# Three reorderings in a hybrid attention and ConvFFN step: page sums of two jobs, page maxima, convolution constants

## The chip, the cores and the metric

The kernel runs on one NeuronCore of a Trainium2 chip, in one launch. The metric is the device time of an execution in microseconds, as the median of several. The engines are named as the profile names them: PE is TensorE, PEld its weight loads, DVE is VectorE, ACT is ScalarE, POOL is GpSimd, SP is SyncE, which here issues all DMAs.

## What is computed

One decoder layer, for a prompt of 1024 tokens and for 8 single new tokens that attend to 1024 past positions each, in float32. The past keys and values lie in 128-row pages that a page table names.

```python
h = _rmsnorm(xp, attn_pre_g[l])
q1, q2, ka, va, qf, kf, vf, logf = _project(h, w_in[l], b_f[l], pos_p)   # rotary on q1, q2, ka
cf = jnp.cumsum(logf, axis=1)
oa, of = _prompt_attention(q1, q2, ka, va, qf, kf, vf, cf, lam)
# oa: (softmax(q1 k1^T) - lam * softmax(q2 k2^T)) v, causal, 4 heads
# of: softmax(q k^T + C[t] - C[s]) v, causal, 8 heads
xp = xp + _rmsnorm(_merge(oa, of, subln_g[l], lam_init, w_o[l]), attn_post_g[l])
xp, conv_p = _conv_ffn(xp, prev0, ffn_pre_g[l], w_gate[l], w_up[l], conv_w[l],
                       conv_b[l], w_down[l], ffn_post_g[l])
...
def _conv_ffn(x, prev, pre_g, w_gate, w_up, conv_w, conv_b, w_down, post_g):
    h = _rmsnorm(x, pre_g)
    g = h @ w_gate
    u = h @ w_up
    gp = jnp.concatenate([prev.astype(g.dtype), g], axis=1)
    c = conv_b
    for j in range(CONV_W):
        c = c + conv_w[j] * gp[:, j:j + S]
    a = jax.nn.gelu(c, approximate=True) * u
    out = a @ w_down
    return x + _rmsnorm(out, post_g), gp[:, -(CONV_W - 1):]
```

The 8 new tokens go through the same steps, with the pages' rows ahead of their own key and value.

## The kernel before

There are three phases: `project` (the input projection, the attention of the prompt and that over the pages), `merge` (output projection and norms) and `ffn`. Every float32 product of the dense layers is made from high and low parts, three products each (`w_hi`, `w_lo`, `ht_hi`, `ht_lo`). In each phase every engine has a program of its own, in a fixed order, and waits on semaphores. The order written in the loops is the order of execution on that engine, and whatever stands behind a waiting instruction waits too.

**The attention loop.** 64 jobs `J`: eight units (head pairs) `u = J // 8` by eight query tiles `t = J % 8`. Units 0 to 3 are the differential group, 4 to 7 the forgetting group (`fox`). A job's steps are spread over the next ones. In job J TensorE makes the scores of J (`scores_of`), one half chunk of a later unit's projection (`before`, twelve products of L1244), transposes of rows for the outputs (`rows_at`: values in tiles 0 and 1, "s" in tile 2, keys "k" in tiles 3 and 4), the weighted sum of J-2 (L1386, L1383), the small products for the page attention (`soft_at`), one or two value pages (L1428), a second half chunk in tiles 0 to 3 (`after`) and at last the transposes of job J-1's probabilities (`turn`, L1370). VectorE takes the maxima of job J's scores (`maximum`, L1103), scales and combines the probabilities of J-1 (`weights`, L1070 to L1079), scales the output rows of J-2 (`rows_out`, L1092, L1089), and does the page work. ScalarE makes the exponentials and copies results out of PSUM.

**The transposes' banks.** All small results of TensorE in this loop go in turn to two PSUM banks, in the order of the list `ring`. An entry may be written when the one two places before it has been copied out. `X` is an entry's place.

**The pages.** 64 key pages in 8 batches. SyncE loads page g (`load_key_page`, L493) into buffer g % 2 once page g-2 is summed (`red_done`); GpSimd multiplies it by the query (`multiply`, L634); VectorE sums it per head (`reduce_page`, L1027). Pages 9 and 10 have their products in job 5, page 11 in job 6, page 12 in job 7. `late_page` marks page 10, whose sum stands in job 7 behind the scaled rows. The others' sums stand at the end of a job, in `pages_and_norms`, with the maxima of a batch (`page_maxima`, L1033 and L1037) after its last page. In soft_at, "mt" transposes those maxima (L1402) one job later, "nm" spreads them to all partitions (L1405) the job after; "ls" sums the denominators (L1410), once, in job 59. VectorE answers with `row_maximum` and `shift`. "mt" falls in jobs 5, 12, 19, 26, 33, 40, 47 and 55, "nm" in the next ones.

**The ConvFFN.** For each of 22 column blocks f TensorE multiplies by gate and up weights. The first three (`PLAIN`) are plain, the rest go by seven half-size products that need sums and differences of the tokens (`token_sums`, on VectorE, spread over f = 0 to 2). Weights of f+1 are split by ScalarE (`split_hi`) and VectorE (`low_parts`). The convolution's taps, bias and state rows and the last norm's gains come as rows and are transposed on TensorE (L2524, L2526) into bank 6, and VectorE copies them out as `consts`.

Of the kernel before, what the change touches and what calls it, by code (L numbers as in the profile page):

```python
# [23 lines left out]
KC = D // P  # L24
# [12 lines left out]
FC = FF // P  # L37
# [125 lines left out]
def project(nc, io, place):  # L163
# [82 lines left out]
    PS = io["PS"]  # L246
# [33 lines left out]
    NJ = MAPS * NT  # L280
# [149 lines left out]
    with nc.Block() as block:  # L430
# [500 lines left out]
        def _(dve):  # L931
# [196 lines left out]
            def pages_and_norms(J):  # L1128
# [3 lines left out]
                for b in at_job(J, 1):  # L1132
                    page_maxima(b)

            behind_first = [4 * NT + NT - 1, 5 * NT + NT - 1, 6 * NT + NT - 1]
            for J in range(NJ + 3):
# [16 lines left out]
                if 2 <= J < NJ + 2 and not fox(J - 2):  # L1153
                    rows_out(J - 2)
                for g in k_pages(J - 2):
                    if late_page(g):
                        reduce_page(g)
# [27 lines left out]
                for b in at_job(J, 5):  # L1185
                    sums(b)
                if J not in behind_first:
                    pages_and_norms(J)
# [33 lines left out]
        def _(pe):  # L1222
# [221 lines left out]
            for J in range(NJ + 3):  # L1444
# [17 lines left out]
                if 2 <= J < NJ + 2:  # L1462
                    weighted_sum(J - 2)
                if J < NJ:
                    for e in soft_at(J):
                        if e[0] != "fb":
                            soft(e)
                    for g in v_pages(J):
                        value_page(g)
                for c, half in after:  # L1470
                    chunk(c, (half,))
                for b in at_job(J, 1):
                    soft(("fb", b))
# [371 lines left out]
def ffn(nc, io, place):  # L1845
# [147 lines left out]
    with nc.Block() as block:  # L1993
# [224 lines left out]
        def _(dve):  # L2218
# [130 lines left out]

            dve.wait_ge(cst_t, 1)  # L2350
            dve.tensor_copy(consts[:, :], PS[:, 6, 0:FC * NR + KC]).then_inc(cst_done, 1)
            dve.wait_ge(cst_done, 1)
            for f in range(FC):
# [20 lines left out]
                if n < FC:  # L2374
                    low_parts(n, 1)
                if f >= PLAIN:
                    combine(f, U3)
# [34 lines left out]
        def _(pe):  # L2412
# [106 lines left out]
            for f in range(PLAIN):  # L2519
                for up in range(2):  # L2520
                    plain(f, up)
                    if f == 0 and not up:
                        pe.wait_ge(rows_ready, 64)
                        pe.transpose(PS[:, 6, FC * NR:FC * NR + KC], g_rows[0:KC, :], ident[0:KC, 0:KC])  # L2524
                        for n in range(FC):
                            ins = pe.transpose(PS[:, 6, n * NR:(n + 1) * NR], rows_in[0:NR, n * P:(n + 1) * P], ident[0:NR, 0:NR])  # L2526
                        ins.then_inc(cst_t, 1)
# [81 lines left out]
```

## Time and profile before

| what | value |
|---|---|
| median of 3 runs | 1476.36 us (1474.67 to 1478.72) |
| profiled execution: time, span | 1474.57 us, 1472.8 us |
| TensorE busy | 1425.4 us, 97% of the span |
| VectorE busy | 861.4 us, 58% |
| ScalarE busy | 638.6 us, 43% |
| GpSimd busy | 366.4 us, 25% |
| granted TensorE clock, mean | 0.994 |
| DMA | 209.91 MB, 143 GB/s in the mean |

The span is the time from the first instruction to the last; the device time has about 1.8 us more around it. Busy time is that in which an engine's instructions run. Of TensorE the page models the ends, so a busy row is not full speed; the granted clock (PEclk) of a stretch says what part of full speed the chip allowed: 1.00 is 2.4 GHz, 0.50 is 1.2 GHz.

### The profile page before, as it was taken

What the parts mean: (1) busy time and instruction counts of PE and PEld (TensorE: products, weight loads), DVE (VectorE), ACT (ScalarE), POOL (GpSimd) and SP (SyncE); (2) the same over time, 40 slices, a digit from 0 to 9 for tenths busy, and PEclk for the clock granted to TensorE, in tenths of its full rate; (3) what the DMA queues carried; (4) which work ended last, traced back from release to release, by engine and by line L of the source; (5) the groups of instructions that cost most, each with busy time, mean ns of one, the idle gap of its engine ahead of it and who ended that gap; (6) DMA issues with size and microseconds to landing.
All of it is one profiled execution on the core that took longest, in us unless ns stands there. A gap on an engine that the chain in (4) does not pass through costs nothing. (4 is left out here: it accounts for less than half of the span.)

```text
span 1472.8 us, 26781 instructions
## 1 busy us (share of the span) xinstructions
PE 1425.4 (97%) x10372; PEld 1287.4 (87%) x10372; DVE 861.4 (58%) x1380; ACT 638.6 (43%) x1198; POOL 366.4 (25%) x545
## 2 busy tenths in 40 slices
PE   7999989999999998799999999999999999999998
PEld 6999877777777775577899999999999999999998
DVE  6421667666565554565449766776666754544663
ACT  6733655544455454343324432333322333433543
POOL 5213876756555550051100000000000000000120
PEclk9999999999999999999999999999999999999999
DMA  6113566778776655331322122222222146665773
GB/s 188 45 49 88 168 183 214 223 221 248 240 220 207 211 172 188 101 114 60 100 80 73 58 87 87 75 84 67 78 87 87 59 158 198 204 190 182 238 256 113
DMA packets 174840, 209.91 MB, mean 143 GB/s; under 512 B 22051, under 2 KB 118891, under 8 KB 174676
## 3 DMA queue, kind: packets, MB, share of 16 engines
q1 hardware_dynamic: 174714, 208.21, 45.4%
q8 instruction: 82, 1.34, 0.4%
q14 instruction: 44, 0.36, 0.1%
HBM read 178.37 MB, written 29.88 MB: 141 GB/s over the span
## 5 line engine op out<-in xcount | busy, mean ns | idle before, releaser
L634 POOL TENSOR_TENSOR k_page<-k_page,q_bc 128x256 f32<-128x256 f32 x256 | 183.7, 749 | 135.7 <-DMA k_page<-in_cache_fox_k 99.2
L1244 PE MATMUL PS<-ht_hi,w_hi 128*128 128x344 f32 x576 | 194.0, 337 | 2.6 <-DVE ht_lo L940 1.4
L1244 PE MATMUL PS<-ht_hi,w_lo 128*128 128x344 f32 x576 | 184.8, 321 | 0.0
L1244 PE MATMUL PS<-ht_lo,w_hi 128*128 128x344 f32 x576 | 184.5, 320 | 0.0
L2482 PE MATMUL PS<-act_hi,wd_hi 128*128 128x344 f32 x528 | 169.1, 320 | 2.8 <-DVE act_lo L2317 2.8
L2482 PE MATMUL PS<-act_hi,wd_lo 128*128 128x344 f32 x528 | 168.6, 319 | 0.0
L2482 PE MATMUL PS<-act_lo,wd_hi 128*128 128x344 f32 x528 | 168.4, 319 | 0.0
L2314 DVE TENSOR_TENSOR wd_lo<-wd_raw,wd_hi 128x1024 fp32r<-128x1024 f32 (+1 forms) x88 | 88.3, 1006 | 114.8 <-ACT act_hi L2125 94.7
L853 ACT ACTIVATE probs<-probs,stat 128x256 f32<-128x256 f32 (+7 forms) x128 | 98.5, 771 | 96.5 <-DVE stat L1103 95.9
L2122 ACT ACTIVATE wd_hi<-wd_raw 128x1024 fp32r<-128x1024 f32 (+1 forms) x88 | 74.2, 845 | 142.0 <-DMA act_raw<-a_dram 106.0
L1244 PEld LDWEIGHTS PS<-ht_hi,w_hi 128*128 128x128 f32 x576 | 109.0, 189 | 28.6 <-issue 21.2
L2437 PE MATMUL PS<-ht_hi,wgu_hi 128*128 128x258 f32 x608 | 122.6, 283 | 0.0
L2437 PE MATMUL PS<-ht_hi,wgu_lo 128*128 128x258 f32 x608 | 122.5, 283 | 0.0
L2437 PE MATMUL PS<-ht_lo,wgu_hi 128*128 128x258 f32 x608 | 122.5, 283 | 0.0
L2108 ACT ACTIVATE conv<-gate,conv_consts 128x1032 f32<-128x1032 f32 x22 | 27.6, 1253 | 207.4 <-DVE gate L2279 185.8
L2085 POOL COPY gate_tails<-gate 128x10 f32<-128x10 f32 x22 | 6.4, 291 | 439.6 <-DVE gate L2279 391.4
L1244 PEld LDWEIGHTS PS<-ht_lo,w_hi 128*128 128x128 f32 x576 | 108.9, 189 | 0.0
L1244 PEld LDWEIGHTS PS<-ht_hi,w_lo 128*128 128x128 f32 x576 | 108.8, 189 | 0.0
L2482 PEld LDWEIGHTS PS<-act_hi,wd_hi 128*128 128x128 f32 x528 | 99.2, 188 | 4.0 <-DVE act_lo L2317 3.9
L1027 DVE TENSOR_REDUCE scores<-k_page 128x16 f32<-128x1024 f32 x64 | 77.5, 1211 | 39.5 <-POOL k_page L634 39.3
L2482 PEld LDWEIGHTS PS<-act_lo,wd_hi 128*128 128x128 f32 x528 | 99.3, 188 | 0.0
L2482 PEld LDWEIGHTS PS<-act_hi,wd_lo 128*128 128x128 f32 x528 | 99.0, 188 | 0.0
(283 smaller groups left out, 3293.0 us busy)
## 6 DMA issues: line engine op xcount, KB each, us to landing
wd_raw<-in_w_down SPq DMA_DIRECT2D x44, 512.0 KB, 3.6
k_page<-in_cache_diff_k SPq DMA_DIRECT2D x64, 256.0 KB, 3.0
k_page<-in_cache_fox_k SPq DMA_DIRECT2D x64, 256.0 KB, 3.5
v_page<-in_cache_diff_v SPq DMA_DIRECT2D x64, 256.0 KB, 2.9
v_page<-in_cache_fox_v SPq DMA_DIRECT2D x64, 256.0 KB, 3.3
w_raw<-in_w_in SPq DMA_DIRECT2D x24, 512.0 KB, 5.0
a_dram<-conv SPq DMA_DIRECT2D x22, 516.0 KB, 3.1
act_raw<-a_dram SPq DMA_DIRECT2D x66, 172.0 KB, 3.7
```

The lines of the kernel that those rows point to most:

```text
L634: ins = pool.tensor_tensor(kpage[:, g % 2, c:c + PIECE], kpage[:, g % 2, c:c + PIECE], qbc[:, c:c + PIECE], ALU.mult)
L853: act.activation(p, p, ACT.Exp, bias=stat[:, J % 8, m:m + 1], scale=-1.0, accum_out=stat[:, J % 8, 2 + m:3 + m]).then_inc(exp_done, 1)
L1027: dve.tensor_reduce(scores[:, b % 3, :, n, :], kpage[:, g % 2, :].rearrange("p (k m c) -> p k m c", k=2, c=HD), AX, ALU.add).then_inc(red_ ...
L1244: ins = pe.matmul(PS[:, z_bank(c), 0:THIRD], b[:, k, :], a[:, k, third(i)], start=(k == 0 and p == 0), stop=(k == KC - 1 and p == 2))
L2085: pool.tensor_copy(tails[:, f, :], gb[:, f % 2, SEQ:SEQ + DB + 2]).then_inc(tail_done, 1)
L2108: act.activation(cbuf[:, f % 2, :], gb[:, f % 2, 2:2 + TOK], ACT.Identity, bias=bias[:, f:f + 1], scale=taps[2][:, f:f + 1]).then_inc(c_in ...
L2122: act.activation(wd_hi[s % NW][:, c], wd_raw[s % NW][:, c], ACT.Copy).then_inc(down_high, 1)
L2314: dve.tensor_tensor(wd_lo[s % NW][:, c], wd_raw[s % NW][:, c], wd_hi[s % NW][:, c].bitcast(F32), ALU.subtract).then_inc(down_low, 1)
L2437: ins = pe.matmul(PS[:, bank + piece, 0:PART], w[:, k, :], a[:, k, piece * PART:(piece + 1) * PART], start=first and k == 0 and m == 0, st ...
L2482: ins = pe.matmul(PS[:, cell_bank(p, d), 0:THIRD], w[:, c], a[:, :], start=f == 0 and m == 0, stop=f == LAST and m == 2, skip_group_check= ...
```

## The change

It has three parts, and no instruction is added or taken away.

1. On VectorE, the page work that stood at the end of jobs 4 and 6 stands in jobs 5 and 7, behind the scaled rows. In job 4 that is page 7's sum with batch 0's maxima, in job 6 page 9's sum.
2. On TensorE, in jobs whose rows_at has a "k" or an "s" (tiles 2, 3 and 4), "mt", "nm" and "ls" stand behind the value pages and the second half chunk.
3. In the ConvFFN the transposes of the constants stand behind the second product group of f = 0 on TensorE, and their copy on VectorE behind both low parts of f = 1.

```diff
--- before.py
+++ after.py
@@ -1132,6 +1132,7 @@
                 for b in at_job(J, 1):
                     page_maxima(b)
 
+            behind_rows = [4, 6]
             behind_first = [4 * NT + NT - 1, 5 * NT + NT - 1, 6 * NT + NT - 1]
             for J in range(NJ + 3):
                 if J >= 3 and fox(J - 3):
@@ -1152,6 +1153,8 @@
                     weights(J - 1)
                 if 2 <= J < NJ + 2 and not fox(J - 2):
                     rows_out(J - 2)
+                if J - 1 in behind_rows:
+                    pages_and_norms(J - 1)
                 for g in k_pages(J - 2):
                     if late_page(g):
                         reduce_page(g)
@@ -1184,7 +1187,7 @@
                             dve.tensor_copy(l_all[0:DB, :], bank_of(e)[0:DB, 2 * MAPS:4 * MAPS]).then_inc(dve_evac, 1)
                 for b in at_job(J, 5):
                     sums(b)
-                if J not in behind_first:
+                if J not in behind_first + behind_rows:
                     pages_and_norms(J)
                 if J in turn_jobs:
                     turned_lo(*turn_jobs[J])
@@ -1461,14 +1464,20 @@
                         turn_rows(e)
                 if 2 <= J < NJ + 2:
                     weighted_sum(J - 2)
-                if J < NJ:
+                behind_chunk = J < NJ and any(e[0] in "ks" for e in rows_at(J))
+                if J < NJ and not behind_chunk:
                     for e in soft_at(J):
                         if e[0] != "fb":
                             soft(e)
+                if J < NJ:
                     for g in v_pages(J):
                         value_page(g)
                 for c, half in after:
                     chunk(c, (half,))
+                if behind_chunk:
+                    for e in soft_at(J):
+                        if e[0] != "fb":
+                            soft(e)
                 for b in at_job(J, 1):
                     soft(("fb", b))
                 if 1 <= J <= NJ:
@@ -2347,9 +2356,6 @@
                     dve.wait_ge(scaled_done, t - EARLY + 1)
                     dve.scalar_tensor_tensor(out[0:n, t % OS, :], y_of(t), stat[0:n, 2, t:t + 1], xr[0:n, t % OS, :], ALU.mult, ALU.add).then_inc(out_late, 1)
 
-            dve.wait_ge(cst_t, 1)
-            dve.tensor_copy(consts[:, :], PS[:, 6, 0:FC * NR + KC]).then_inc(cst_done, 1)
-            dve.wait_ge(cst_done, 1)
             for f in range(FC):
                 n = f + 1
                 if f > PLAIN:
@@ -2373,6 +2379,10 @@
                     multiply(f - 1)
                 if n < FC:
                     low_parts(n, 1)
+                if f == 0:
+                    dve.wait_ge(cst_t, 1)
+                    dve.tensor_copy(consts[:, :], PS[:, 6, 0:FC * NR + KC]).then_inc(cst_done, 1)
+                    dve.wait_ge(cst_done, 1)
                 if f >= PLAIN:
                     combine(f, U3)
                 if PLAIN <= n < FC:
@@ -2519,7 +2529,7 @@
             for f in range(PLAIN):
                 for up in range(2):
                     plain(f, up)
-                    if f == 0 and not up:
+                    if f == 0 and up:
                         pe.wait_ge(rows_ready, 64)
                         pe.transpose(PS[:, 6, FC * NR:FC * NR + KC], g_rows[0:KC, :], ident[0:KC, 0:KC])
                         for n in range(FC):
```

VectorE, jobs 6 to 8 of the attention loop; first of before, from the shift of batch 0's scores (L1053, job 6) to job 8's maximum (the row of 128x128). L1027 are page sums, ISA L1103 the score maxima.

```order
L1053 TENSOR_TENSOR scores_99<-scores_99,PS 128x64 x2
L1027 TENSOR_REDUCE scores_99<-k_page_95 128x2x8
L1103 ISA probs_77,stat_106<-PS,zeros_mask_86 128x1024
L1103 ISA stat_106 128x1
L1103 ISA probs_77,stat_106<-PS,zeros_mask_86 128x1024
L1103 ISA stat_106 128x1
L1070 RECIPROCAL stat_106<-stat_106 128x2
L1075 TENSOR_SCALAR stat_106<-stat_106,small_51 128x1
L1079 SCALAR_TENSOR_TENSOR probs_77<-probs_77,stat_106 128x896
L1092 TENSOR_SCALAR q_t_64<-PS,stat_106 128x128
L1027 TENSOR_REDUCE scores_99<-k_page_95 128x2x8 x2
L1103 ISA probs_77,stat_106<-PS,zeros_mask_86 128x128
```

```order
L1053 TENSOR_TENSOR scores_99<-scores_99,PS 128x64 x2
L1103 ISA probs_77,stat_106<-PS,zeros_mask_86 128x1024
L1103 ISA stat_106 128x1
L1103 ISA probs_77,stat_106<-PS,zeros_mask_86 128x1024
L1103 ISA stat_106 128x1
L1070 RECIPROCAL stat_106<-stat_106 128x2
L1075 TENSOR_SCALAR stat_106<-stat_106,small_51 128x1
L1079 SCALAR_TENSOR_TENSOR probs_77<-probs_77,stat_106 128x896
L1092 TENSOR_SCALAR q_t_64<-PS,stat_106 128x128
L1027 TENSOR_REDUCE scores_99<-k_page_95 128x2x8 x3
L1103 ISA probs_77,stat_106<-PS,zeros_mask_86 128x128
L1103 ISA stat_106 128x1
```

The sum that stood in job 6 ahead of job 7's maxima is now the first of three in a row, behind job 5's scaled rows (L1092) and ahead of job 8's maximum; the second is page 10's, the third page 11's.

TensorE, job 12 (unit 1, tile 4), from the transposes of key rows to the next job's scores; first before, then after, where the same steps have line numbers 3 higher. `page_max` is "mt", `v_page` the value page, `probs` the transposes of job 11's probabilities.

```order
L1358 MATMUL PS<-ident_50,k_t_70 128x128 x4
L1386 MATMUL PS<-v_rows_72,a_t_80 128x128 x3
L1402 MATMUL PS<-ident_50,page_max_122 16x128
L1428 MATMUL PS<-v_page_98,scores_99 4x256 x4
L1370 MATMUL PS<-ident_50,probs_77 128x128 x4
L1334 MATMUL PS<-k_t_70,q_t_64 128x512 x2
L1334 MATMUL PS<-k_t_70,q_t_64 128x256 x2
```

```order
L1361 MATMUL PS<-ident_50,k_t_70 128x128 x4
L1389 MATMUL PS<-v_rows_72,a_t_80 128x128 x3
L1431 MATMUL PS<-v_page_98,scores_99 4x256 x4
L1405 MATMUL PS<-ident_50,page_max_122 16x128
L1373 MATMUL PS<-ident_50,probs_77 128x128 x4
L1337 MATMUL PS<-k_t_70,q_t_64 128x512 x2
L1337 MATMUL PS<-k_t_70,q_t_64 128x256 x2
```

The transpose of the page maxima has moved behind the value page. In jobs 19, 26, 27 and 34 it or its follower moves behind twelve weight products as well.

TensorE, start of the ConvFFN; first before, then after. `wgu_hi_10949` and `wgu_lo_10950` are the weights of f = 0, `wgu_hi_10952` those of f = 1; `g_rows` and `rows_in` the constants.

```order
L1548 MATMUL PS<-ht_lo_63,wgu_hi_10949 128x344
L1548 MATMUL PS<-ht_hi_62,wgu_lo_10950 128x344
L2524 MATMUL PS<-ident_50,g_rows_12267 128x8
L2526 MATMUL PS<-ident_50,rows_in_12169 128x20 x22
L1548 MATMUL PS<-ht_hi_62,wgu_hi_10949 128x344
```

```order
L1557 MATMUL PS<-ht_lo_63,wgu_hi_10949 128x344
L1557 MATMUL PS<-ht_hi_62,wgu_lo_10950 128x344
L2534 MATMUL PS<-ident_50,g_rows_12267 128x8
L2536 MATMUL PS<-ident_50,rows_in_12169 128x20 x22
L1557 MATMUL PS<-ht_hi_62,wgu_hi_10952 128x344
```

Before, the constants' transposes stood between two product groups of f = 0; now they stand between f = 0 and f = 1.

## Rows read from the trace of the kernel before

**Rows 1.** Waits of TensorE by releaser: us in total, times, longest.
```profile
PE PS L1402 <- ACT k_rows L841: 2.1, 2, 1.3
PE PS L2524 <- DMA g_rows<-in_ffn_post_g: 1.5, 1, 1.5
...
PE PS L1402 <- ACT sample_rows L830: 0.7, 1, 0.7
...
PE PS L1405 <- ACT k_rows L841: 0.5, 2, 0.3
```

**Rows 2.** TensorE's timeline, jobs 5 to 8: start us, us, instruction, idle before.
```profile
179.71 1.56 PE L1334 MATMUL PS<-k_t,q_t 64*128 64x512 f32 x8
...
186.08 0.74 PE L1370 MATMUL PS<-ident,probs 128*128 128x128 f32 x5 [1.73 <-DVE q_t L1092]
186.75 1.77 PE L1334 MATMUL PS<-k_t,q_t 64*128 64x512 f32 x8
...
193.71 0.85 PE L1370 MATMUL PS<-ident,probs 128*128 128x128 f32 x6 [1.66 <-DVE q_t L1092]
...
208.59 1.04 PE L1370 MATMUL PS<-ident,probs 128*128 128x128 f32 x8
```

**Rows 3.** VectorE's timeline, jobs 4 to 8.
```profile
180.70 1.22 DVE L1027 TENSOR_REDUCE scores<-k_page 128x16 f32<-128x1024 f32 x1 [1.24 <-POOL k_page L634]
...
182.53 0.95 DVE L1103 CUSTOM_DVE_ANT_0 probs<-PS,zeros_mask 128x768 f32<-128x768 f32 x1
...
185.59 0.35 DVE L1092 TENSOR_SCALAR q_t<-PS,stat 128x128 f32<-128x128 f32 x1
...
189.51 1.08 DVE L1103 CUSTOM_DVE_ANT_0 probs<-PS,zeros_mask 128x896 f32<-128x896 f32 x1
...
196.61 1.22 DVE L1103 CUSTOM_DVE_ANT_0 probs<-PS,zeros_mask 128x1024 f32<-128x1024 f32 x1 [1.66 <-PE PS L1334]
...
200.75 1.21 DVE L1027 TENSOR_REDUCE scores<-k_page 128x16 f32<-128x1024 f32 x1
204.17 1.22 DVE L1027 TENSOR_REDUCE scores<-k_page 128x16 f32<-128x1024 f32 x1 [2.21 <-POOL k_page L634]
...
208.00 0.34 DVE L1092 TENSOR_SCALAR q_t<-PS,stat 128x128 f32<-128x128 f32 x1
```

**Rows 4.** SyncE's queue: second halves of pages 11 and 12 issued.
```profile
196.90 0.34 SPq L493 DMA_DIRECT2D k_page<-in_cache_fox_k  x1
...
202.56 0.38 SPq L493 DMA_DIRECT2D k_page<-in_cache_fox_k  x1
```

**Rows 5.** GpSimd's timeline: page products of pages 11, then 12 and 13.
```profile
201.33 2.81 POOL L634 TENSOR_TENSOR k_page<-k_page,q_bc 128x256 f32<-128x256 f32 x4 [4.00 <-DMA k_page<-in_cache_fox_k]
205.58 6.56 POOL L634 TENSOR_TENSOR k_page<-k_page,q_bc 128x256 f32<-128x256 f32 x8 [1.45 <-DMA k_page<-in_cache_fox_k]
```

**Rows 6.** TensorE's timeline in the last unit, its longest wait in the loop.
```profile
600.85 0.33 PE L1370 MATMUL PS<-ident,probs 128*128 128x128 f32 x1 [2.52 <-DVE q_t L1089]
```

**Rows 7.** Windows of TensorE: us, busy (x), PEclk, DMA share, GB/s.
```profile
182.50:189.30 6.80, 5.07 (x33) 1.00 0.55 166
602.30:605.70 3.40, 3.40 (x28) 0.50 0.04 10
762.80:769.60 6.80, 6.80 (x30) 0.50 0.34 94
```

**Rows 8.** TensorE's timeline in job 59.
```profile
580.24 0.54 PE L1410 MATMUL PS<-ones_sq,l_parts 128*16 128x1 f32 x16 [0.19 <-ACT k_rows L841]
581.38 0.61 PE L1428 MATMUL PS<-v_page,scores 128*4 128x256 f32 x8 [0.61 <-DMA v_page<-in_cache_fox_v]
```

**Rows 9.** TensorE's timeline, the transposes of the convolution's rows.
```profile
761.79 1.82 PE L2526 MATMUL PS<-ident,rows_in 20*128 20x20 f32 x22
```

**Rows 10.** VectorE's timeline at the start of the ConvFFN.
```profile
766.30 1.22 DVE L1531 TENSOR_TENSOR wgu_lo<-wgu_raw,wgu_hi 128x1024 fp32r<-128x1024 f32 x1 [2.03 <-ACT wgu_hi L1528]
```

**Rows 11.** Window of VectorE: us, busy (x), PEclk, DMA share, GB/s.
```profile
766.30:820.80 54.50, 51.40 (x38) 0.97 0.23 68
```

## The prediction

> **What bounds the kernel now.** I read the busy shares first (the table ahead): TensorE has work in 97% of the span, 1425.4 of 1472.8 us. An edit on another engine counts only where TensorE stands idle behind it, and its 47.4 idle us are the whole stock from which this change can earn. So TensorE's waits by releaser come next [rows 1]: 2.1 + 0.7 us at the page-maximum transposes of L1402 behind ScalarE's row copies, 0.5 at their broadcasts of L1405, 1.5 for the DMA of g_rows. Then the timelines of the places, because a wait removed on one engine may come back on another. Jobs 5 to 8 of the attention loop run from 181 to 209 us.
>
> **First part, job 4's page work.** Before, VectorE waits until 180.70 for page 7's product, sums it, adds the gate sums, takes the maxima, and starts job 5's score maximum only at 182.53, 1.83 later [rows 3], although TensorE ended those scores (L1334) at 179.71 + 1.56 = 181.27 [rows 2]. Moved, the score maximum starts at 181.4 (0.14 is the step from VectorE's end, 185.59 + 0.35, to TensorE's start at 186.08), 1.1 us earlier, and so do job 3's scaled rows: 185.59 becomes 184.5. But job 5's transpose of page maxima (L1402) is queued on TensorE ahead of the transposes of L1370. It now waits for sum, add and maxima: 184.5 + 0.26 to the next start + 1.9 + 0.14 = 186.8. TensorE, done with its weighted sum at 184.2 (0.1 before L1402 ended, which is 186.08 less 1.73), is idle 2.55 us instead of 1.73, and L1370 starts at 187.0 instead of 186.08. The next scores end at 189.45, not 188.52, and job 6's maximum starts at 189.6 instead of 189.51, because VectorE is held there by page 8's sum in both kernels. The wait of 1.66 us in job 6 [rows 2] eats the loss. Price of this half: 0.1 us.
>
> **First part, job 6's page work.** Moving page 9's sum (1.2 us) gives nothing back: VectorE idles 1.66 us behind it, until TensorE's scores come, ahead of 196.61 [rows 3]. What it costs is a buffer. Pages alternate between two buffers, and SyncE's load of page 11 (L493) waits until page 9 is summed. Before, its second half was issued at 196.90, and GpSimd began its product at 201.33 [rows 4, 5]. Now page 9's sum takes the place of page 10's, at 200.75. Its end is exactly where page 12's load is released in the kernel before: second half issued at 202.56, product begun at 205.58 [rows 4, 5]. So page 11's product now runs from 205.6 for 2.81 us, and its sum, at 204.17 in [rows 3], starts at 208.4: 4.25 us later. VectorE works in order: behind this sum stand job 8's maxima, job 7's probabilities and job 6's scaled rows, which ended at 208.00 + 0.34. TensorE took them at 208.59 (L1370, [rows 2]) and could have at 208.48, so 0.1 of the shift is hidden: an idle stretch of 4.1 us. Pages 10 and 12 have their data in time, and from job 9 on every load has its old distance again, so nothing is given back.
>
> **Clock.** After an idle 2.52 us ahead of 600.85 [rows 6] the granted clock is 0.50, the 1.2 GHz level, from 602.3 to 605.7 [rows 7]; that costs half of 3.4 us. Job 8's idle stretch is longer and TensorE is the bound behind it: 1.7 us (bounds 0 and 3.4). Job 5's 2.55 us lies between that case and the 1.73 us around which the clock stayed at 1.00 (182.5 to 189.3, [rows 7]); a fall would double the 1.2 us or so of transposes and scores that set job 6's start: bounds 0 and 1.2, taken 0.6, since neither row is clearly nearer.
> The Trainium skill (TensorE: Matmul & The Clock Gate, section "Why this matters for your kernels") warns of throughput drops after long idle gaps between bursts; taken for job 8's gap alone, the sum would be 0.6 less. The fall behind 2.52 us here says that a shorter gap can do it too.
>
> **Second part.** The test for "k" and "s" holds in tiles 2, 3 and 4. There lie six transposes or broadcasts (L1402 in jobs 12, 19 and 26, L1405 in 20, 27 and 34) and the denominators' sum (L1410) in job 59. The six wait for a bank that ScalarE's row copy frees. Now a value page (0.61 us, the duration at 581.38 in [rows 8]) and, outside tile 4, twelve weight products run first. So the waits of [rows 1] end unnoticed: 2.1 + 0.7 + 0.5 = 3.3, less 0.1 that the one value page of job 12 leaves uncovered. VectorE gets the maxima up to 2 us later; it idles about as long for TensorE's next scores, which covers it (1.66 in [rows 3] is such a wait). Job 59 loses: its value page waits for a DMA until 581.38, and L1410 (0.54 us) was hidden ahead of it; now it comes behind. Sum: -3.3 + 0.1 + 0.5 = -2.7. Bounds -3.3 (job 59's hidden after all) and -1.9 (VectorE's lateness passed on in two jobs, 0.4 each).
>
> **Third part.** TensorE's 1.5 us for g_rows [rows 1] go, since the rows land while 24 products run. But the products after them, of f = 1, need low parts that VectorE makes from 766.30 on, held by ScalarE and a load and not by TensorE: the first is done at 767.5 [rows 10]. Products now end at 763.8, the narrow transposes (1.82 us, [rows 9]) at 765.6, and TensorE waits 2.0 us: first product of f = 1 at 767.6. Before, it started at 770.1, since behind 1.5 idle and 1.8 of narrow transposes, 3.6 together with the gaps, the clock was 0.50 from 762.8 to 769.6 [rows 7], at a cost of (769.6 - 763.6)/2 = 3.0. The new stretch of transposes and idle is 3.85 us, so I expect the same fall: 0.2 slower. With half of it the part is 1.3 faster; with none 2.5, which VectorE allows only just: it is idle 3.1 us in the stretch to 820.8 [rows 11], and the constants' copy, 0.6, now stands ahead of the token sums. Bounds -2.5 and +0.9 (a longer fall), taken +0.2.
> The Trainium skill (same page, Part 4) says that transposes do not count as TensorE work for the clock in the same way; by it the new stretch falls like the old, and the 0.50 of [rows 7] agrees.
>
> **Sum.** 0.1 + 0.6 + 4.1 + 1.7 - 2.7 + 0.2 = +4.0 us. The profiled execution took 1474.57 us (span 1472.8), 1.8 below the median of 1476.36; it would be 1478.6, and the median 1480.4. About 0.3%, 4.4 us, is what a measurement of this kernel can tell from no change.
>
> **Rivals.**
> Slower by a late landing: from issue to product page 11 took 4.43 us before, page 12 3.02 [rows 4, 5], and now a 512 KB weight load follows page 11 at once. At 4.43 job 8 idles 5.5: sum +5.4, 1481.8. It decides from 0.4 us above page 12's figure. Against it: the value pages that ran beside page 11 before are gone by then. Chance 0.20.
> Slower by the clock: job 5's fall in full, or a second one in job 8: +4.6 to +5.7, 1481.0 to 1482.1. For it the 2.52 us case, against it the 1.73. Chance 0.20.
> No stall in job 8: page 11's product is not what VectorE stands for. Then only -2.7 + 0.2 + 0.7, or less with the third part's gain: -1.8 to -4.5, 1474.6 to 1471.9. Against it is VectorE's row of three sums. Chance 0.13, of which 0.09 beyond 0.3%.
> No fall in the third part: 4.0 - 2.7 = +1.3, 1477.7. Chance 0.10.
> My forecast has 0.37.
>
> **Numbers.** Forecast, no fall and 0.04 of "no stall" are within 0.3%: 0.51. The two slower rivals make 0.40, the rest 0.09. For the range: lowest sum with the stall and no fall in job 8 4.1 - 3.3 - 2.5 + 0.7 = -1.0; highest 5.5 + 3.4 + 1.3 - 1.9 + 0.2 = +8.5, cut to 7.6 as it needs all at once. 1475.4 to 1484.0.
>
> **What will show it.** Right: three page sums in a row on VectorE, the third behind a wait for GpSimd; TensorE idle near 4 us ahead of the transposes (L1373) after 208, and a clock of 0.50 behind; no waits left at L1405 in jobs 12, 19 and 26; TensorE waiting for wgu_lo near 766. Wrong: page 11's product begun before 204, a clock of 1.00 around 763 to 770, or waits that reappear at L1373 in jobs 20, 27 or 35.

## The result, and the profile of the changed kernel

| | before | changed |
|---|---|---|
| median of 11 runs each, in turn | 1476.41 us (1474.67 to 1480.76) | 1480.53 us (1476.70 to 1484.03) |
| ratio, 95% interval | | 1.0026 (1.0014 to 1.0039) |
| profiled execution, its span | 1474.57, 1472.8 us | 1476.70, 1474.7 us |
| mean granted clock of the profiled execution | 0.994 | 0.993 |

The kernel became slower by some 4 us, as forecast. The changed kernel's profiled execution is the lowest of its eleven, so the two traces differ by only 2.1 us where the medians differ by 4.1. Most of the rest is the clock: the share of the span that it took (span times 1 minus clock) is 10.3 us in this execution and 13.9 on the average of the eleven, against 8.8 in the trace of before and 10.8 on the average of the 91 runs of before that stand beside the experiments below (its own eleven list no clock). A turn is a transpose on TensorE. In the changed kernel L1405 is the turn of the page maxima (L1402 before), L1408 the row maxima (L1405), L1373 the turn of the probabilities (L1370), L1247 the weight chunks (L1244), L1431 the page of values (L1428), L1557, L2447, L2492 the ConvFFN's products.

TensorE's waits by releaser in the changed kernel (us in total, times, longest), beside [rows 1]:
```profile
PE PS L1373 <- DVE q_t L1089: 5.1, 4, 2.5
PE PS L1373 <- DVE probs L1079: 5.0, 5, 3.8
...
PE PS L1405 <- DVE page_max L1037: 2.5, 1, 2.5
PE PS L1431 <- DMA v_page<-in_cache_fox_v: 2.2, 2, 1.5
...
PE PS L1247 <- POOL w_lo L604: 1.9, 4, 0.9
...
PE PS L1557 <- ACT gate L2187: 1.5, 1, 1.5
...
PE PS L1399 <- POOL lf_after L645: 0.9, 2, 0.6
...
PE PS L1405 <- ACT k_rows L841: 0.4, 1, 0.4
```
Of the waits for ScalarE's rows at the maxima, 3.3 us before in [rows 1] and 3.5 with a sixth of 0.2, 0.4 is left. In their place stand one wait for a page maximum, one of 3.8 for VectorE's probabilities, and two small entries that count GpSimd (low parts of weights, gate sums of later pages).

TensorE's timeline in jobs 5 to 8, beside [rows 2]:
```profile
186.21 0.28 PE L1405 MATMUL PS<-ident,page_max 128*16 128x128 f32 x1 [2.53 <-DVE page_max L1037]
...
192.99 0.85 PE L1373 MATMUL PS<-ident,probs 128*128 128x128 f32 x6 [0.59 <-DVE q_t L1092]
...
211.77 1.45 PE L1373 MATMUL PS<-ident,probs 128*128 128x128 f32 x8 [3.76 <-DVE probs L1079]
```
VectorE, GpSimd and SyncE's queue over the same jobs, beside [rows 3 to 5]:
```profile
184.16 1.21 DVE L1027 TENSOR_REDUCE scores<-k_page 128x16 f32<-128x1024 f32 x1
...
185.77 0.38 DVE L1037 TENSOR_REDUCE page_max<-scores 128x16 f32<-128x128 f32 x1
...
200.02 2.33 DVE L1027 TENSOR_REDUCE scores<-k_page 128x16 f32<-128x1024 f32 x2
207.85 1.22 DVE L1027 TENSOR_REDUCE scores<-k_page 128x16 f32<-128x1024 f32 x1 [5.50 <-POOL k_page L634]
208.99 0.28 DVE L1103 CUSTOM_DVE_ANT_0 probs<-PS,zeros_mask 128x128 f32<-128x128 f32 x1
...
209.91 1.81 DVE L1079 SCALAR_TENSOR_TENSOR probs<-probs,stat 128x1024 f32<-128x1024 f32 x1
```
```profile
205.02 2.80 POOL L634 TENSOR_TENSOR k_page<-k_page,q_bc 128x256 f32<-128x256 f32 x4 [7.02 <-DMA k_page<-in_cache_fox_k]
```
```profile
201.87 0.34 SPq L493 DMA_DIRECT2D k_page<-in_cache_fox_k  x1
```
Read it from the bottom. The second half of page 11 is issued at 201.87, 4.97 us later than before (196.90), because the sum of the page whose buffer it takes now ends at about 201.2. GpSimd's product starts at 205.02 (201.33 before), 3.15 us behind the issue, close to the 3.02 of page 12 in [rows 4, 5]; so the rival of a late landing did not come true. VectorE, in order, has three page sums in a row, and stands 5.50 us at the third with job 8's maxima and probabilities queued behind it. TensorE has nothing for 3.76 us.

Windows of TensorE (us, busy, granted clock, DMA share, GB/s) behind that stall, around the transposes of the convolution's constants, and late in the ConvFFN, beside [rows 7]:
```profile
212.60:216.00 3.40, 3.40 (x13) 0.53 0.71 222
216.00:219.40 3.40, 3.40 (x32) 1.00 0.13 49
...
763.00:769.80 6.80, 5.84 (x51) 1.00 1.00 266
...
1400.50:1403.90 3.40, 3.40 (x14) 0.54 1.03 413
```
The granted clock falls to the lower level (1.2 GHz) behind the idle of 3.76 us and is back at the higher one (2.4 GHz) by 216.0. Around 766, where before had 6.8 us of low clock, there is none, and it falls once near 1400, where before it did not.

The start of the ConvFFN's second weights, beside [rows 9]:
```profile
767.24 0.22 PE L2534 MATMUL PS<-ident,g_rows 8*128 8x8 f32 x1
767.33 1.52 PE L2536 MATMUL PS<-ident,rows_in 20*128 20x20 f32 x22
770.37 0.40 PE L1557 MATMUL PS<-ht_hi,wgu_hi 128*128 128x344 f32 x1 [1.52 <-ACT gate L2187]
```

How far the changed kernel lags behind before, at the same instruction of TensorE in both traces:

| place | before | changed | lag |
|---|---|---|---|
| job 7's turn | 200.62 | 199.90 | −0.7 |
| job 8's turn | 208.59 | 211.77 | +3.2 |
| job 15's turn | 256.79 | 261.11 | +4.3 |
| job 31's turn | 370.84 | 372.87 | +2.0 |
| behind job 59's page of values | 584.50 | 587.94 | +3.4 |
| products ahead of the constants | 756.18 | 759.53 | +3.4 |
| first product of the second weights | 770.13 | 770.37 | +0.2 |
| behind VectorE's first u | 824.47 | 825.12 | +0.6 |
| end of the span | 1472.8 | 1474.7 | +1.9 |

### The profile page after: what moved, and what is told of

It reads as the page before. It is cut to its first block and busy times, and to the rows that moved or that the text cites. A ratio compares the mean times of both kernels' runs of the same rounds, so it can differ in the third digit from the quotient of the medians.

```text
span 1474.7 us, 26780 instructions
## 1 busy us (share of the span) xinstructions
PE 1424.6 (97%) x10372; PEld 1285.8 (87%) x10372; DVE 863.8 (59%) x1380; ACT 638.8 (43%) x1198; POOL 365.6 (25%) x545
## 2 busy tenths in 40 slices
DMA packets 174840, 209.91 MB, mean 142 GB/s; under 512 B 22051, under 2 KB 118891, under 8 KB 174676
## 5 line engine op out<-in xcount | busy, mean ns | idle before, releaser
L1247 PE MATMUL PS<-ht_hi,w_hi 128*128 128x344 f32 x576 | 194.2, 337 | 4.0 <-POOL w_lo L604 1.9
L1247 PE MATMUL PS<-ht_hi,w_lo 128*128 128x344 f32 x576 | 184.9, 321 | 0.0
L1247 PE MATMUL PS<-ht_lo,w_hi 128*128 128x344 f32 x576 | 184.7, 321 | 0.0
L2492 PE MATMUL PS<-act_hi,wd_hi 128*128 128x344 f32 x528 | 169.7, 321 | 2.8 <-DVE act_lo L2326 2.8
L2492 PE MATMUL PS<-act_hi,wd_lo 128*128 128x344 f32 x528 | 169.3, 321 | 0.0
L2492 PE MATMUL PS<-act_lo,wd_hi 128*128 128x344 f32 x528 | 169.1, 320 | 0.0
L1247 PEld LDWEIGHTS PS<-ht_hi,w_hi 128*128 128x128 f32 x576 | 109.1, 189 | 30.2 <-issue 21.5
L2447 PE MATMUL PS<-ht_hi,wgu_hi 128*128 128x258 f32 x608 | 122.6, 283 | 0.0
L2447 PE MATMUL PS<-ht_hi,wgu_lo 128*128 128x258 f32 x608 | 122.5, 283 | 0.0
L2447 PE MATMUL PS<-ht_lo,wgu_hi 128*128 128x258 f32 x608 | 122.5, 283 | 0.0
L1247 PEld LDWEIGHTS PS<-ht_lo,w_hi 128*128 128x128 f32 x576 | 109.1, 189 | 0.0
L1247 PEld LDWEIGHTS PS<-ht_hi,w_lo 128*128 128x128 f32 x576 | 109.0, 189 | 0.0
L2492 PEld LDWEIGHTS PS<-act_hi,wd_hi 128*128 128x128 f32 x528 | 99.7, 189 | 3.8 <-DVE act_lo L2326 3.7
L2492 PEld LDWEIGHTS PS<-act_lo,wd_hi 128*128 128x128 f32 x528 | 99.8, 189 | 0.0
L1027 DVE TENSOR_REDUCE scores<-k_page 128x16 f32<-128x1024 f32 x64 | 77.4, 1211 | 38.2 <-POOL k_page L634 38.0
L2492 PEld LDWEIGHTS PS<-act_hi,wd_lo 128*128 128x128 f32 x528 | 99.6, 189 | 0.0
```

The source lines that it names most:

```text
L1027: dve.tensor_reduce(scores[:, b % 3, :, n, :], kpage[:, g % 2, :].rearrange("p (k m c) -> p k m c", k=2, c=HD), AX, ALU.add).then_inc(red_ ...
L1247: ins = pe.matmul(PS[:, z_bank(c), 0:THIRD], b[:, k, :], a[:, k, third(i)], start=(k == 0 and p == 0), stop=(k == KC - 1 and p == 2))
L2447: ins = pe.matmul(PS[:, bank + piece, 0:PART], w[:, k, :], a[:, k, piece * PART:(piece + 1) * PART], start=first and k == 0 and m == 0, st ...
L2492: ins = pe.matmul(PS[:, cell_bank(p, d), 0:THIRD], w[:, c], a[:, :], start=f == 0 and m == 0, stop=f == LAST and m == 2, skip_group_check= ...
```

## The experiments

Ten kernels, in three comparisons, each beside runs of the kernel before on the same chip. Since times of the same kernel spread by some 5 us to either side, the mean granted clock of each run is read too: span times (1 minus clock) is how much full-speed time the low clock took (a run's clock is given to 0.001, which is 1.5 us, so only means are used).

| kernel | median us | of before | ratio (95%) | mean low-clock cost, us |
|---|---|---|---|---|
| changed | 1480.53 | 1476.41 | 1.0026 (1.0014 to 1.0039) | 13.9 |
| part one alone | 1482.77 | 1477.67 | 1.0041 (1.0027 to 1.0056) | 14.5 |
| job 6's move alone | 1482.86 | 1477.67 | 1.0042 (1.0028 to 1.0056) | 13.2 |
| part two alone | 1475.61 | 1477.67 | 0.9992 (0.9974 to 1.0011) | 12.3 |
| part three alone | 1476.17 | 1477.67 | 0.9994 (0.9982 to 1.0007) | 9.8 |
| job 4's move alone | 1476.64 | 1476.94 | 0.9997 (0.9983 to 1.0010) | 11.8 |
| jobs 4, 6 and 7 moved | 1480.55 | 1476.94 | 1.0027 (1.0012 to 1.0042) | 12.6 |
| parts two and three | 1474.53 | 1476.94 | 0.9980 (0.9968 to 0.9993) | 11.1 |
| the same, weights first | 1475.38 | 1476.94 | 0.9983 (0.9970 to 0.9996) | 10.4 |
| changed, job 6 undone | 1477.39 | 1476.70 | 1.0000 (0.9985 to 1.0014) | 12.5 |
| parts two and three, low parts first | 1472.80 | 1476.70 | 0.9973 (0.9960 to 0.9986) | 10.8 |

The kernel before, in the 91 of these runs that list a clock, has a mean time of 1476.9 us and a low-clock cost of 10.8 us.

**Part one alone.**
```diff
+            behind_rows = [4, 6]
+                if J - 1 in behind_rows:
+                    pages_and_norms(J - 1)
-                if J not in behind_first:
+                if J not in behind_first + behind_rows:
```


> First part alone (page work of jobs 4 and 6 behind the scaled rows), the rest as before. My theory: the whole loss of the change is here. TensorE idle 3.8 to 4.2 us ahead of L1370 in job 8, 2.5 ahead of L1402 in job 5, clock 0.50 once behind job 8; time +4.5 to +6.5 us over before (ratio 1.0030 to 1.0044). Rival: the loss comes from elsewhere (more clock falls by chance, the third part); then this kernel is within 2 us of before.

Measured: the ratio is 1.0041, 5.1 us by the medians. In its trace TensorE waits 2.47 us for the page maximum in job 5, 0.58 in job 6, and 3.34 for the probabilities in job 8, with the low clock behind that. The whole loss of the changed kernel is in part one.

**Job 6's move alone.**
```diff
+            behind_rows = [6]
```


> Only job 6's page sum is moved. My theory: page 11's load waits for page 9's sum, so all of job 8's idle stretch of 3.8 to 4.2 us is still there, and job 5 is as before (idle 1.7 us ahead of L1370): +4.5 to +6 us. Rival: job 8's stall needs job 4's move too, because that makes page 9's product late as well; then TensorE's idle in job 8 is under 1 us and the time is within 1.5 us of before.

Measured: 1.0042, the same as both moves together. TensorE's waits in its jobs 5, 6, 7 and 8:
```profile
187.18 0.74 PE L1373 MATMUL PS<-ident,probs 128*128 128x128 f32 x5 [0.42 <-DVE q_t L1092]
194.47 0.30 PE L1373 MATMUL PS<-ident,probs 128*128 128x128 f32 x1 [1.32 <-DVE q_t L1092]
...
201.38 0.98 PE L1373 MATMUL PS<-ident,probs 128*128 128x128 f32 x7 [0.71 <-DVE probs L1079]
...
213.04 1.97 PE L1373 MATMUL PS<-ident,probs 128*128 128x128 f32 x8 [3.52 <-DVE probs L1079]
```
The stall in job 8 needs nothing of job 4. Here 6.8 us at the low clock lie around and behind it (windows of TensorE):
```profile
211.90:218.70 6.80, 5.66 (x22) 0.52 0.66 203
215.30:218.70 3.40, 3.40 (x14) 0.53 0.48 129
218.70:222.10 3.40, 3.40 (x33) 1.00 0.10 39
```

**Job 4's move alone.**
```diff
+            behind_rows = [4]
```


> Part one with job 4 alone: the page sum of job 4 stands behind job 5's scaled rows, that of job 6 stays where it was. Theory (the whole loss of the changed kernel is the sum of job 6): TensorE waits 2.4 to 2.6 us for VectorE's page maximum in job 5, which takes the place of the 1.73 and of the wait of 1.66 in job 6, and job 8 has no wait over 1 us ahead of the query's turn, as before. The time is within 1 us of the kernel before (1476.4 to 1478.7 beside its 1477.7). Rival (a page sum behind the scaled rows costs wherever it is put): 2 us or more above the kernel before, and a wait for VectorE of over 2 us in job 6 or 7. Second rival (job 4 is a gain of its own that job 6 hid): 1 us or more below.

Measured: 0.9997, 0.3 us under before. TensorE's waits in jobs 5 and 6:
```profile
189.18 0.28 PE L1405 MATMUL PS<-ident,page_max 128*16 128x128 f32 x1 [2.80 <-DVE page_max L1037]
...
197.18 0.85 PE L1373 MATMUL PS<-ident,probs 128*128 128x128 f32 x6 [0.21 <-DVE q_t L1092]
```
The later stall takes the place of the two waits of [rows 2]. The first rival (a place behind the rows costs anywhere, 2 us or more) falls. The second (a gain of 1 us or more that job 6 hid) is not seen, but the interval reaches 2.5 us below before and does not exclude it. This move delays a load too: page 9's second half is issued at 188.67 (183.25 before), and GpSimd waits 2.83 us for it. But VectorE sums page 9 only at 197.27 (193.75 before), behind its product at 191.46 to 194.25, so this delay is covered. The place of a page sum is indifferent as long as the delay of the next load is covered.

**Page 11's sum moved as well.** If VectorE's order alone costs, issuing the late sum later must cure it.
```diff
+            behind_rows = [4, 6, 7]
```


> As the changed kernel's part one, but page 11's sum is also issued one place later, behind the scaled rows of job 8 instead of ahead of them. Theory (VectorE works in order, and stands 5.50 us at page 11's sum for its product, with job 8's scaled rows and probabilities queued behind it): TensorE's idle of 3.3 to 3.8 us ahead of the query's turn in job 8 falls under 1 us, the low clock behind it is gone, and the time comes back to within 1.5 us of the kernel before. Rival (the late landing of page 11 itself is what costs, and a later place only moves the stall): TensorE waits 2 us or more for VectorE in job 8's maximum or in job 9, and the time stays 3 us or more above the kernel before.

Measured: 1.0027, 3.6 us over before. The stall in job 8 is gone, and so is the low clock behind it (1.00 in all of 208 to 216); TensorE's rows run through it. But three jobs on, at job 11's first weight chunk, TensorE waits for ScalarE, ScalarE for GpSimd, and GpSimd has come from four page products that each waited for their load (TensorE, ScalarE, then GpSimd):
```profile
229.22 0.40 PE L1247 MATMUL PS<-ht_hi,w_hi 128*128 128x344 f32 x1 [2.70 <-ACT z_raw L742]
```
```profile
228.61 0.46 ACT L742 ACTIVATE z_raw<-PS 128x344 f32<-128x344 f32 x1 [5.03 <-POOL k_t L661]
```
```profile
207.56 2.81 POOL L634 TENSOR_TENSOR k_page<-k_page,q_bc 128x256 f32<-128x256 f32 x4 [8.34 <-DMA k_page<-in_cache_fox_k]
...
220.01 3.00 POOL L634 TENSOR_TENSOR k_page<-k_page,q_bc 128x256 f32<-128x256 f32 x4 [2.05 <-DMA k_page<-in_cache_fox_k]
222.98 2.81 POOL L604 TENSOR_TENSOR w_lo<-w_raw,w_hi 128x256 fp32r<-128x256 f32 x4
...
227.61 0.91 POOL L661 TENSOR_TENSOR k_t<-z_raw,z_swapped 128x344 f32<-128x344 f32 x1
```
So my theory holds in the place and fails in the cause: VectorE's order decides which engine meets the late page, and the lateness itself, made by the sum that frees the buffer, is what costs. The rival foresaw the moved stall and the time, but looked for it on VectorE in jobs 8 or 9; it came out on GpSimd's queue, and on TensorE in job 11.

**Part two alone.**
```diff
-                if J < NJ:
+                behind_chunk = J < NJ and any(e[0] in "ks" for e in rows_at(J))
+                if J < NJ and not behind_chunk:
...
+                if behind_chunk:
+                    for e in soft_at(J):
```
(exactly as in the changed kernel, job 59 with it)


> Second part alone. My theory: 2.5 to 2.9 us faster than before (ratio 0.9981): the six waits of L1402 and L1405 for ScalarE's copies are gone, job 59 has an idle stretch of about 1.3 us ahead of its first value page. Rival: the waits come back as waits for low weight parts (L604) or for the page products, since GpSimd and the page chain have their own pace; then under 1.5 us faster.

Measured: 0.9992, an interval that holds both 1 and the expectation. Its low-clock cost is 12.3 us against 10.8, with an error of about 1 on twelve runs, which would hide some 1.5 us of gain but is not certain. In its trace the six waits are down to 0.2 us, and job 59's value page is waited for 1.39 us (0.61 before), as expected. The rival's waits are there too: 3.2 us for low parts where before has 1.0. Of these 1.88 stand at 17.5 us and are in job 4's move alone as well (1.87), so they are not part two's; 0.50 at 397, and 0.43 and 0.32 for the gate sums at 378 and 486, stand where before has 0.43 in all. Inconclusive by itself.

**Part three alone.**
```diff
-            dve.wait_ge(cst_t, 1)
-            dve.tensor_copy(consts[:, :], ...)
...
+                if f == 0:
+                    dve.wait_ge(cst_t, 1)
+                    dve.tensor_copy(consts[:, :], ...)
...
-                    if f == 0 and not up:
+                    if f == 0 and up:
```


> Third part alone. Forecast as on record: 0.2 us slower, because TensorE's wait for low parts (2.0 us) takes the place of that for g_rows and the granted clock falls to 0.50 for 6.8 us as before. Rival, which the changed kernel's profile supports: the stretch of narrow transposes and idle brings no fall, the first product of f = 1 starts 2.5 to 3 us earlier and about 2.5 of it is left at the end: 2 to 3 us faster. If both happen by turns, single times spread over 3 us or more.

Measured: 0.9994, 1.5 us under by the medians and 0.6 by the means (1476.23 against 1476.86). The first product of the second weights waits 1.25 us, and the clock does fall behind it in this profile, for 3.4 us instead of 6.8. The time lies between the forecast's +0.2 and the rival's −2.5.

**Parts two and three, without part one.** This and the two kernels built on it also keep the old order in job 59 (`LS`), where the denominators' sum stays ahead of the value pages. Against the changed kernel:
```diff
-            behind_rows = [4, 6]
...
-                behind_chunk = J < NJ and any(e[0] in "ks" for e in rows_at(J))
+                behind_chunk = J < NJ and J != LS and any(e[0] in "ks" for e in rows_at(J))
```


> Parts two and three without part one, and without job 59's weight chunk in part two. By the medians of the two parts alone (2.1 and 1.5 us below the kernel before in their own comparison) they add up to 3.6 us below, ratio 0.9976; by the profiled traces (2.0 to 3.3 and 2.7) to 4.7 to 6, ratio 0.996 to 0.997. Theory: the gains add, since they lie in different stages, and the ratio is 0.996 to 0.998 with an interval that leaves out 1. Rival (what part two wins is given back at the weights' own arrivals): ratio 0.999 or above, with waits of TensorE for weight chunks of 0.3 us or more in jobs 15, 19 and 26 to 29.

Measured: 0.9980 (0.9968 to 0.9993), 2.4 us under before, which fits gains that add, at the smaller of the two sizes. It is no clean sum: job 59's value page is waited for 0.71 us here, 1.39 in part two alone. The rival's waits are there as well, only small (two for weights, one for the gate sums):
```profile
338.35 0.42 PE L1244 MATMUL PS<-ht_hi,w_hi 128*128 128x344 f32 x1 [0.44 <-POOL w_lo L604]
...
395.93 0.42 PE L1244 MATMUL PS<-ht_hi,w_hi 128*128 128x344 f32 x1 [0.38 <-POOL w_lo L604]
485.83 0.41 PE L1396 MATMUL PS<-lf_pages,suffix 128*128 128x64 f32 x2 [0.61 <-POOL lf_after L645]
```

**The same, weights first.**
```diff
+            for up in range(2):
+                load_weights(sp, 1, up)
             (loads of the constants' rows)
-            for up in range(2):
-                load_weights(sp, 1, up)
```


> As p23, and SyncE issues the two loads of the second part's first weights ahead of the loads of the constants' rows. Theory (in part three the wait of 1.2 to 1.5 us ahead of the second part's first product is what the weights' arrival leaves, and the constants' rows stand in front of them in SyncE's queue): that wait falls under 0.8 us, and the time is 0.4 to 1 us under that of p23. Rival (ScalarE's or VectorE's chain on the gate sets the start of the second part): the wait is unchanged, the time within 0.4 us of p23. Second rival: the constants' rows land later, their turn on TensorE waits, and the time is above p23's.

Measured: 0.9983, no different from the kernel above. TensorE's rows above are of parts two and three, those below of this kernel:
```profile
764.94 0.22 PE L2531 MATMUL PS<-ident,g_rows 8*128 8x8 f32 x1
765.02 1.52 PE L2533 MATMUL PS<-ident,rows_in 20*128 20x20 f32 x22
768.14 0.40 PE L1554 MATMUL PS<-ht_hi,wgu_hi 128*128 128x344 f32 x1 [1.59 <-ACT gate L2184]
```
```profile
766.51 0.22 PE L2531 MATMUL PS<-ident,g_rows 8*128 8x8 f32 x1 [1.43 <-DMA g_rows<-in_ffn_post_g]
766.60 1.52 PE L2533 MATMUL PS<-ident,rows_in 20*128 20x20 f32 x22
```
The wait ahead of the second weights is gone, and one of 1.43 us for the rows stands ahead of the transposes; the products begin at 768.1 in both. The two loads share one queue, and whichever is second is late. The wait went as my theory said, the gain of 0.4 to 1 us did not come. That is my second rival's wait; its loss, 0.85 us by the medians and 0.4 by the means, is too small to be told from nothing here.

**The changed kernel with job 6 undone.**
```diff
-            behind_rows = [4, 6]
+            behind_rows = [4]
```


> The changed kernel with one part of it undone: job 6's page sum and maxima back ahead of the scaled rows (job 4's stay behind them), parts two and three as changed. Theory (the loss of the changed kernel is the sum of job 6 alone, and parts two and three win together what they win without part one): ratio 0.997 to 0.999, an interval that leaves out 1, within 1.5 us of the kernel with parts two and three alone (ratio 0.998), and no wait of TensorE over 1 us between the ends of jobs 6 and 10. Rival (the parts hinder each other, and part of the 2.6 per thousand lies in their sum): ratio 0.9995 or above.

Measured: 1.0000 (0.9985 to 1.0014). Undoing this one list entry gives back the changed kernel's loss of 2.6 in a thousand. The rest of the expectation is missed: 0.998 was to be had without part one. Its profile has low clock near 181 and 191, and for 6.8 us from 771 (windows of TensorE):
```profile
180.70:184.10 3.40, 3.40 (x11) 0.52 0.50 123
190.90:194.30 3.40, 3.40 (x12) 0.51 0.49 133
771.20:778.00 6.80, 6.13 (x22) 0.51 0.15 42
```
Job 4's move alone has the falls near 181 and 191 too, and costs nothing by its times (the one near 181 stands ahead of the moved work, and job 6's move alone has it as well). This kernel differs from parts two and three by job 4's move and by job 59's order: its page of values there is waited for 1.29 us, 0.71 in the other. Whether job 4's move costs 1 us or so beside that, or the difference from 0.998 is scatter (the intervals overlap), stays open.

**Low parts first.** On top of parts two and three, GpSimd makes a weight tile's low parts ahead of the job's page product.
```diff
+                if n < len(TILES) and n != v_tile(1):
+                    split_lo(n)
                 for g in k_pages(J)[:1]:
                     ...
                     multiply(g)
-                if n < len(TILES) and n != v_tile(1):
-                    split_lo(n)
```


> Parts two and three (as in the kernel with those alone), and GpSimd makes the low parts of a weight tile ahead of the page's product of the same job instead of behind it. Theory (what part two wins is partly given back as waits of TensorE for these low parts, 2.1 us in four waits in the profile of parts two and three alone, since GpSimd stands at a page's load with the low parts queued behind it): these waits go to under 0.3 us in total, the page products come 2.8 us later, and the time is 0.5 to 2 us under that of parts two and three alone, ratio 0.9965 to 0.9978. Rival (the page products are the nearer bound: later by 2.8 us they hold VectorE's sums and with them the scaled rows, as page 11's did in job 8): new waits of TensorE for VectorE of 1 us or more in early jobs, and a ratio of 0.999 or above.

Measured: 0.9973 (0.9960 to 0.9986), 3.9 us under before, the fastest kernel here, and not told apart from parts two and three alone with certainty. The three waits shown above are gone; the two at 27 and 50 us, which I had wrongly counted as part two's doing, remain (1.2 us of the 2.1), so "under 0.3 us in total" is missed. GpSimd's queue shows where the low parts go, into the gap in which it used to wait for a page:
```profile
385.36 2.82 POOL L604 TENSOR_TENSOR w_lo<-w_raw,w_hi 128x256 fp32r<-128x256 f32 x4
389.25 2.81 POOL L634 TENSOR_TENSOR k_page<-k_page,q_bc 128x256 f32<-128x256 f32 x4 [1.07 <-DMA k_page<-in_cache_fox_k]
```
The page product waits for its load anyway, and TensorE has no new wait of 1 us for VectorE, so nothing of the rival's is seen.

## Why the prediction was right, and where it was not

1. **Job 5 (+0.1): right.** The stall is 2.53 us (2.55 forecast) in place of 1.73, and job 6 waits 0.59 in place of 1.66; job 7's turn lags by −0.7 (this execution was 0.6 ahead in job 4 already, before the change acts). Job 4's move alone, at 0.9997, confirms it. One reading was off without harm: job 6's maximum starts at 189.03 behind TensorE's scores, not behind page 8's sum, which is done at 188.27.
2. **A low clock behind job 5 (+0.6, a chance): not in the changed kernel's profile.** It is in three others with the same move: the stall is 2.44, 2.80 and 2.82 us there (jobs 4, 6 and 7 moved, job 4's move alone, job 6 undone), 2.53 and 2.47 in the changed kernel and in part one alone, which have none. So a chance was the right form; its cost is not settled (above).
3. **Job 8 (+4.1): right, 3.8 measured.** The idle is 3.76 us, by the chain that the text gives: sum of page 9, load of page 11, GpSimd's product, VectorE's third sum. Job 6's move alone has it all, which confirms the term. The text's 4.1 took TensorE to wait for job 6's scaled rows. In job 8 it waits for job 7's probabilities (L1079) instead: it starts at 211.77, while the scaled rows run from 211.64 for 0.34. These probabilities end 0.3 us earlier (208.08 before, against 208.34), so that more of the shift was hidden than the 0.1 of the text. What the text lacked is that the late load costs in whatever queue meets it: with page 11's sum out of the way, the time stayed 3.6 us above before.
4. **The low clock behind it (+1.7): right, 1.6.** From job 7's lag of −0.7 to +4.8 at job 9's weighted sum are 5.5 us; 3.9 of them are reached at job 8's turn, 1.6 are left. Over all runs the changed kernel's low clock costs 13.9 us against 10.8, with an error of about 1: of some 4 us of loss, some 3 are time at the low clock. That is more than this one fall explains, and no run here divides it.
5. **Part two (−2.7): mis-sized, −1.4 in the trace.** The waits that it was to remove are gone but 0.4 us (job 12), and the lag falls from +4.8 to +2.0. Then 1.0 us comes back up to 500, mostly as waits that TensorE did not have before or had shorter: 0.41 for GpSimd's low parts at 400, and 0.25 at 381 and 0.61 (0.43 before) at 490 for the gate sums (one more of 0.29, for low parts at 342, is already in the +2.0). And 0.5 comes back in job 59, as forecast, where the page of values is now waited for 1.48 and 0.69 us (0.61 in [rows 8]). The forecast took the cover of TensorE's next inputs as free. Low parts first has none of those at 338 to 490.
6. **Part three (+0.2): wrong, −2.7 in the trace, about −0.6 to −1.5 over the runs.** The step that failed is "the same fall": the transposes now stand ahead of a wait of 1.52 us instead of behind one of 1.51, and the clock stayed high, as the rival with a chance of 0.10 had it. From +3.4 to +0.2 are 3.1 us; VectorE's first u, now waited for 0.64 us instead of 0.31, takes back 0.4. But the order does not decide it. Of the six profiles with the new order three fall there (part three alone, parts two and three, job 6 undone) and three do not; of the six with the old order three fall (before, part one alone, jobs 4, 6 and 7 moved) and three do not, beside waits of 1.25 to 1.60 us in the new order and of 1.27 to 1.51 us in the old. So the 3.0 us of low clock in the one trace of before were a chance already in the kernel before, and should have been counted with a chance on both sides. The other half, that the wait merely changes its name, was right, at 1.52 us instead of 2.0. The trace names ScalarE's copy of the gate and not VectorE's low parts as what ended it; both stand behind ScalarE's split of the second weights, which waits for their load until 767.87. And weights first shows that it goes to whichever load is second.
7. **What was not in the sum:** one fall near 1400 in this execution, +1.7. Nothing ties it to the change: of the ten other kernels' profiles six have it, with and without each part.

The sum was +4.0 and the medians say +4.1. In the traces the terms give 5.5 − 1.4 − 2.7 + 1.7, less 0.5 of lag gone between 825 and the end and less the 0.7 at which the comparison starts: +1.9, the difference of the spans. That these traces differ by 1.9 and the medians by 4.1 shows how much single executions scatter.

Over many runs part one costs 6.1 us (1.0041) where the sum had 6.5, which carries the forecast. Parts two and three were to win 2.5 and win 1.2 and 0.9 as single kernels (0.9992 and 0.9994), neither told from nothing. Each of these figures is uncertain by about 2 us, so that the sum comes within 0.1 us of the medians is luck.

## What to carry to other kernels

Before moving an instruction later, ask which buffer it frees: a move that is free on its own engine pushes the next load into that buffer, and where nothing covers the delay (page 9's was covered, page 11's not) the late data stalls whichever in-order queue meets it first (moving the consumer too only changes the engine, here from VectorE to GpSimd). Where a wait on a critical engine is removed, list the inputs that it hid; GpSimd's low parts came out as the next wait, and making them in the gap ahead of a late load gave the fastest kernel here, though not by a clear margin. Where single executions of a kernel spread by more than the effect, average the granted clock over the runs, and don't take a fall of the clock in one trace as a fixed term of the sum.

## What the runs showed of the hardware

- The granted clock goes with much of the spread of one program. Of the 91 runs of the kernel before, the 17 with a mean clock of 0.990 or less took 1479.6 us on average, the 21 with 0.995 or more 1474.0. The same idle brings a fall in one execution and none in another. In job 5 a fall stands behind 2.44 us (jobs 4, 6 and 7 moved: 0.50 from 187.0 to 190.4) and none behind 2.53 (changed: 1.00 from 186.0 to 189.4); one behind 2.19 (part two alone: 0.55 from 187.0 to 190.4) and none behind 2.21 (parts two and three: 1.00 from 187.4 to 190.8).
- VectorE's scaling of 128x1024 took 1.81 us at 209.91 in the changed kernel, while GpSimd multiplied a page from 208.55 on, and 1.28 us at 205.83 in the kernel with jobs 4, 6 and 7 moved, where GpSimd was idle from 199.2 to 207.56. GpSimd's four products at 208.55 took 3.76 us, 2.81 in that other kernel at 207.56. Here the two engines slowed each other, which made job 8's chain half a microsecond longer; it did so before the change as well (1.85 us at 206.23), so it is no part of the difference.
